# A transformer block on one core: the causal convolution by 128-column blocks, 11 of its taps on TensorE, and its layer norm in halves

## The chip, the cores and the metric

The kernel runs on one core of a Trainium2 chip. The metric is the device time of one execution in microseconds (us). The core has five engines that run side by side and meet at semaphores: TensorE (PE), VectorE (DVE), ScalarE (ACT), GpSimd (POOL) and SyncE (SP, which here only issues DMAs).

## The reference

One layer on 512 tokens of width 1024: a convolution branch and an attention branch from one projection, an output projection, and a mixture of 32 experts (each token uses 4).

```
u = rms_norm(x, norm_mix_g)
a, g, q, k, v = split(u @ w_in)                  # a and g: 512 columns each
y = causal_depthwise_conv(a * sigmoid(g), conv_w)    # 31 taps, per channel
conv_out = silu(layer_norm(y + conv_b))          # norm over the 512 channels
attn_out = diff_attention(q, k, v)               # 4 heads, 4 query blocks, 2 maps per head
h = x + concat(conv_out, attn_out) @ w_out
h = h + moe(rms_norm(h, norm_ffn_g))             # router, top 4, two matmuls per expert
```

## The kernel before

**Stages.** The program is written out by hand, engine by engine: each engine has one list of instructions in a fixed order, and semaphores hold it where it needs another's result. There are five stages.

1. *Entry.* x is loaded, normed and turned; `uT_hi` and `uT_lo` are its two parts. Every large product of the kernel is made of three matmuls, high by high, high by low and low by high (`split_mm`, L1374 to L1376), so each weight chunk of 1 MB goes through ACT (`hi_front`, L606, makes `whi`) and DVE (`lo_front`, L920, makes `wlo`) before PE can use it.
2. *Projections.* The chunks c = 0 to 9 of w_in. Chunks 0 and 2 hold the columns of a, 1 and 3 those of g, with 256 columns each, that is two blocks (o = 0 and 1) of 128 channels. The convolution has its channels on the partitions, in four such blocks; a block's gated input is `gated(c)` (L944), which needs the sigmoid on ACT (L632, L637). The four rows of the attention bias are made of the one-hot matrix on PE (`bias_row`, L1387), copied out by ACT (L618, L619), stored and loaded again by SP. Then come v (chunks 4, 5), q (6, 7) and k (8, 9).
3. *Units.* The attention has 16 units, one for each query block qb and head h, with keys of width 128 (units 0 to 3), 256 (4 to 7), 384 (8 to 11) and 512 (12 to 15). In its round i each engine does a fixed list. PE: the scores of unit i + 2 (L1473), then what stands beside unit i, then the transposes of unit i (L1550), then the values of unit i - 1 (L1532). DVE: the row maximum of unit i + 1 (L1037), the sum of one tile if there is one (L1084), the difference of the two maps of unit i (L1047 to L1055), then what stands beside it. ACT: the exponentials of unit i + 1 (L699), the copy of the turned map of unit i (L742), the output of unit i - 1 (L709, L710), then what stands beside it.
4. *Output projection.* The half that multiplies the convolution's output is eight tiles (`tile_of_conv(j)`: chunk 10 for j = 0 to 3, chunk 11 for j = 4 to 7) of 12 matmuls each, every one summed into `h1` by DVE (`add_tile(j)`). The attention's half is `out_rows(t)`, from chunks 12 and 13. Between the last values and `out_rows(0)` stand the deviation of the attention output (L752), its scaling (L1127) and its turning (L1563), split by ACT (L758) and DVE (L1132).
5. *Experts.* Routing, then a loop over expert items, each with 12 chunks of 1 MB.

**The convolution's taps.** A tap of one block on DVE is one instruction over 128 x 512 (L962, the first one of a block L958). `dve_taps` is the order of the taps, and `conv(count)` issues the next `count` of them. On PE a tap is a matmul with a diagonal matrix that ACT makes from the identity (`diagonals`, L626), and it is summed in one bank of PSUM (`conv_taps`, L1459). Before, block 3 has all its 31 taps on PE and blocks 0 to 2 theirs on DVE (93). Both run on into the units: 5 DVE taps beside each of units 0 to 3 and 1 beside unit 4, and `PE_TAPS_BESIDE` = 6, 7, 7, 7, 4 PE taps beside units 0 to 4.

**The layer norm.** Its steps stand beside units, by the constants MEAN to SPLIT: the means on PE (L1485, unit 5), the centring on DVE (L1065, 5), the squares on ACT (L716, 5), the variance on PE (L1492, 6), the deviation on ACT (L720, 6), the reciprocal and the norm on DVE (L1070, L1071, 7), SiLU and the high part on ACT (L725, L728, 7), the low part on DVE (L1075, 8). From unit 9 (`FIRST_TILE`) on one tile stands beside each unit; all but the last use one bank (`SPARE_BANK`), so a tile waits for the sum of the one before. The tile j = 7 stands behind the turning of the attention output. The bias of the experts' first product is prepared beside units 10 (DVE, L1100), 11 (ACT, L692), 12 and 13 (DVE, L1104).

```
        MEAN, CENTRE, SQUARE, VARIANCE, DEVIATION, NORM, SILU, SPLIT, FIRST_TILE = 5, 5, 5, 6, 6, 7, 7, 8, 9
        TAPS_BESIDE = 5
        CONV_BANK = [SPARE_BANK] * (2 * T - 1) + [7]
        PE_TAPS_BESIDE = (6, 7, 7, 7, 4)
```

SP starts to load the experts' weights when the values of the last unit are done.

## Time and profile before

| | us |
|---|---|
| median of 3 runs (lowest, highest) | 1468.08 (1465.13, 1468.4) |
| the profiled execution's own time | 1468.58 |
| its span, first to last instruction | 1467.0 |
| PE, DVE, ACT busy in the span | 1402.7, 1233.8, 1005.5 |
| first matmul of the projections | 19.1 |
| first tap on PE (start of unit 0) | 146.6 |
| first tile | 210.1 |
| end of the last unit's values | 248.2 |
| first transpose of `h1` | 269.6 |

A timeline row gives start, duration, engine, line, operation, what it writes and reads, shape, count, and in brackets how long the engine stood idle before it and who ended that. A row of the chain of waits gives start, duration and what was on the chain. A row of a table by stage gives the stage, then the busy time of PE, PE's weight loads, DVE, ACT and POOL (with the number of instructions), the clock that TensorE was granted as a share of 2.4 GHz, the share of DMA time and GB/s. A grouped row gives the count, the busy time in us, the mean ns of one, and the idle time before.

### The profile page before, as it was taken

To read this page: it belongs to the slowest core of one execution; us is meant where nothing else is said; L and a number is where in the kernel's file an instruction comes from. 1 tells how busy PE (TensorE), PEld (TensorE's weight loads), DVE (VectorE), ACT (ScalarE), POOL (GpSimd) and SP (SyncE) were. 2 spreads that over 40 slices of the span, in tenths; PEclk is the share of its full clock that TensorE was granted. 3 is DMA by queue.
4 is the path that set the end of the run, shared out by engine and by line. 5 is a ranking of instruction groups with operands and counts; after the bars stand their busy time and mean duration, and the time that the engine had idled before them with its cause. 6 is when DMAs were issued, how large, how long until landed. Compare 5 with 4: busy or idle time off the path is not lost.

```text
span 1467.0 us, 20156 instructions
## 1 busy us (share of the span) xinstructions
PE 1402.7 (96%) x6532; PEld 1133.0 (77%) x6532; DVE 1233.8 (84%) x1059; ACT 1005.5 (69%) x1016; POOL 265.4 (18%) x285
## 2 busy tenths in 40 slices
PE   6999968988999999999999999999999999999995
PEld 4887446876788888888888888888888888888884
DVE  4688666488899989999999999998989899899984
ACT  5248365256677777777777777777777777777773
POOL 3000000026221121111211112111121222221111
PEclk9999979999999999999999999999999999999998
DMA  8412002689999999999999999999999999999971
GB/s 245 153 56 86 15 15 74 256 287 203 411 402 391 383 378 370 368 373 371 362 379 370 366 383 361 388 357 366 379 363 372 370 365 376 375 368 370 370 284 21
DMA packets 96969, 446.78 MB, mean 305 GB/s; under 512 B 14896, under 2 KB 19008, under 8 KB 63920
## 3 DMA queue, kind: packets, MB, share of 16 engines
q1 hardware_dynamic: 82944, 422.86, 76.3%
q0 software_dynamic: 12000, 20.49, 5.4%
q10 hardware_dynamic: 2000, 3.10, 0.7%
q8 instruction: 14, 0.23, 0.1%
q14 instruction: 11, 0.09, 0.0%
HBM read 439.70 MB, written 22.43 MB: 315 GB/s over the span
## 4 chain that ended last, share of the span: by engine, by line
PE 91%; DVE 2%; DMA 2%; issue 2%; POOL 1%; ACT 1%; SPq 0%; ACTq 0%; POOLq 0%; DVEq 0%
PE psum L1374 27%; PE psum L1376 27%; PE psum L1375 26%; PE psum L1698 2%; PE psum L1459 2%; PE psum L1707 2%; POOL slot_table L512 1%; PE psum L1724 1%; DMA xg<-hn_rows,slot_i 1%; DMA ring<-in_w_in 1%; PE psum L1594 1%; PE psum L1532 0%; PE psum L1632 0%; PE psum L1473 0%; PE psum L1492 0%
## 5 line engine op out<-in xcount | busy, mean ns | idle before, releaser
L1224 DVE TENSOR_TENSOR wlo<-ring,whi 128x2048 fp32r<-128x2048 f32 x384 | 871.5, 2290 | 101.8 <-ACT whi L792 97.8
L792 ACT ACTIVATE whi<-ring 128x2048 fp32r<-128x2048 f32 x384 | 737.6, 1921 | 197.0 <-PE psum L1376 196.9
L1374 PE MATMUL psum<-whi,xT_hi 128*128 128x512 f32 x1024 | 402.2, 393 | 7.3 <-DVE xT_lo L1230 3.7
L1376 PE MATMUL psum<-wlo,xT_hi 128*128 128x512 f32 x1024 | 398.7, 389 | 0.0
L1375 PE MATMUL psum<-whi,xT_lo 128*128 128x512 f32 x1024 | 398.7, 389 | 0.0
L1374 PEld LDWEIGHTS psum<-whi,xT_hi 128*128 128x128 f32 x1024 | 192.3, 188 | 47.8 <-DVE wlo L1224 5.0
L1376 PEld LDWEIGHTS psum<-wlo,xT_hi 128*128 128x128 f32 x1024 | 192.2, 188 | 40.2
L1375 PEld LDWEIGHTS psum<-whi,xT_lo 128*128 128x128 f32 x1024 | 192.4, 188 | 38.6
L1374 PE MATMUL psum<-whi,aT_hi 128*128 128x512 f32 x512 | 202.6, 396 | 1.9 <-ACT y_sb L845 1.9
L1376 PE MATMUL psum<-wlo,aT_hi 128*128 128x512 f32 x512 | 200.0, 391 | 0.0
L1375 PE MATMUL psum<-whi,aT_lo 128*128 128x512 f32 x512 | 200.0, 391 | 0.0
L533 POOL DMA_INDIRECT out<-y_sb,slots x32 | 81.1, 2533 | 398.5 <-ACT y_sb L845 385.1
L1374 PEld LDWEIGHTS psum<-whi,aT_hi 128*128 128x128 f32 x512 | 96.6, 189 | 21.3 <-issue 2.2
L1376 PEld LDWEIGHTS psum<-wlo,aT_hi 128*128 128x128 f32 x512 | 96.4, 188 | 20.2
L1375 PEld LDWEIGHTS psum<-whi,aT_lo 128*128 128x128 f32 x512 | 96.5, 189 | 19.2
L545 POOL COPY slots_moved<-slots 128x4 int32<-128x4 int32 x30 | 30.0, 1002 | 265.9 <-DMA out<-y_sb,slots 265.9
L1374 PE MATMUL psum<-whi,uT_hi 128*128 128x512 f32 x160 | 65.2, 407 | 4.4 <-DVE uT_lo L1075 2.2
L832 ACT ACTIVATE sig<-psum 128x512 f32<-128x512 f32 x64 | 34.7, 594 | 48.4 <-PE psum L1724 48.4
L504 POOL DMA_INDIRECT xg<-hn_rows,slots x30 | 34.0, 1133 | 177.6 <-PE psum L1698 142.4
L1376 PE MATMUL psum<-wlo,uT_hi 128*128 128x512 f32 x160 | 63.7, 398 | 0.0
L1375 PE MATMUL psum<-whi,uT_lo 128*128 128x512 f32 x160 | 63.5, 397 | 0.0
L838 ACT ACTIVATE aT_hi<-psum 128x512 fp32r<-128x512 f32 x64 | 34.8, 596 | 41.2 <-PE psum L1707 41.2
(256 smaller groups left out, 1342.2 us busy)
## 6 DMA issues: line engine op xcount, KB each, us to landing
ring<-in_w_gate_up SPq DMA_DIRECT2D x256, 1024.0 KB, 7.9
ring<-in_w_down SPq DMA_DIRECT2D x128, 1024.0 KB, 7.2
ring<-in_w_in SPq DMA_DIRECT2D x10, 1024.0 KB, 12.0
ring<-in_w_out SPq DMA_DIRECT2D x4, 1024.0 KB, 5.0
h<-in_x SPq DMA_DIRECT2D x4, 512.0 KB, 5.5
hn_rows<-hn ACTq DMA_DIRECT2D x4, 512.0 KB, 2.6
out<-h POOLq DMA_DIRECT2D x4, 512.0 KB, 11.1
bias_rows<-rows_st SPq DMA_DIRECT2D x1, 1280.0 KB, 4.8
```

The costliest lines, as they stand in the source:

```text
L504: pool.indirect_dma_start(out=xg[:, :], out_offset=None, in_=hn_rows, in_offset=bass.IndirectOffsetOnAxis(ap=index, axis=0), bounds_check= ...
L533: pool.indirect_dma_start(out=out, out_offset=bass.IndirectOffsetOnAxis(ap=slots[:, place, 0:1], axis=0), in_=y_sb[:, :], in_offset=None, ...
L545: COPY(slots_moved[:, :, token], slots[:, 1:5, token]).then_inc(move_step, 1)
L792: nc.scalar.activation(whi[:, hi_of(number), :], ring[:, slot(number), :], ACT.Copy).then_inc(hi_ready, 1)
L832: nc.scalar.activation(sig[:, cols], bank(2 * half, 2).rearrange("p (f two) -> p two f", two=2)[:, 0, :], ACT.Silu, scale=ALPHA).then_inc( ...
L838: nc.scalar.activation(aT_hi[:, half * 4:half * 4 + 4, :], bank(6 + half), ACT.Copy, scale=1.0 / ALPHA).then_inc(aT_hi_done, 1)
L1224: TT(wlo[:, slot(number), :], ring[:, slot(number), :], whi[:, hi_of(number), :].bitcast(F32), ALU.subtract).then_inc(lo_ready, 1)
L1374: MM(o, s_hi, m_hi, start=first, stop=False)
L1375: MM(o, s_lo, m_hi, start=False, stop=False)
L1376: return MM(o, s_hi, m_lo, start=False, stop=last)
L1459: ins = MM(bank(SPARE_BANK), diag[:, n, :], u_pad[:, 3, n:n + S], start=(n == 0), stop=(n == PE_TAPS - 1))
L1698: ins = nc.tensor.transpose(bank(6 + half)[:, k * P:(k + 1) * P], xg[:, (half * 4 + k) * P:(half * 4 + k + 1) * P], ident[:, :])
```

## The change

**a and g by blocks.** PE no longer takes chunk by chunk but block by block: a's block 0, g's block 0, a's block 1, g's block 1, then the bias rows, then the same for blocks 2 and 3. ACT's sigmoids and DVE's `gated` follow one by one, and DVE's taps start right behind the first. `dve_taps` gets a new order (block 0 alone for 13 taps, then pairs of neighbouring blocks). SP's load of chunk 6 stands behind the bias rows as before.

**11 taps of block 3 on PE, 20 on DVE.** `PE_TAPS` goes from 31 to 11 (the last 11 taps), 3, 3, 3 and 2 beside units 0 to 3. DVE has 113 taps; 4 beside each of units 0 to 2, the other 9 beside unit 3, where the bank of PE's taps is added too.

**The layer norm** stands beside later units, and centring, squares, norm, SiLU, high and low parts are done for tokens 0 to 255 and 256 to 511 one after the other: means at unit 5, centring 6, squares 7, variance and deviation 9, norm 10 and 11, SiLU 12, low part 13. **The tiles** start at unit 14: tiles 0 and 1 stand beside units 14 and 15, the other six between the last values and the turning of the attention output, over three banks. Chunk 12's low part is made among their sums, chunk 13's high part behind the deviation of the attention output. **The up bias's steps** stand beside units 11, 13, 14 and 15.

```diff
-PE_TAPS = TAPS
+PE_TAPS = 11
...
-        MEAN, CENTRE, SQUARE, VARIANCE, DEVIATION, NORM, SILU, SPLIT, FIRST_TILE = 5, 5, 5, 6, 6, 7, 7, 8, 9
-        TAPS_BESIDE = 5
-        CONV_BANK = [SPARE_BANK] * (2 * T - 1) + [7]
-        PE_TAPS_BESIDE = (6, 7, 7, 7, 4)
+        CONV_END, MEAN, CENTRE, SQUARE, VARIANCE, DEVIATION, NORM, SILU, SPLIT, FIRST_TILE = 3, 5, 6, 7, 9, 9, 10, 12, 13, 14
+        TAPS_BESIDE = 4
+        HALVES = (slice(0, S // 2), slice(S // 2, S))
+        BESIDE_TILES = H * T - FIRST_TILE
+        CONV_BANK = [SPARE_BANK] * BESIDE_TILES + [(SPARE_BANK, 6, 7)[j % 3] for j in range(2 * T - BESIDE_TILES)]
+        PE_TAPS_BESIDE = (3, 3, 3, 2)
...
+                for half, cols in enumerate(HALVES):
+                    act.wait_ge(normed, half + 1)
+                    for c in range(4):
+                        nc.scalar.activation(ln_tmp[:, c, cols], acc[:, c, cols], ACT.Silu, bias=ln_b[:, c:c + 1],
+                                             scale=ln_g[:, c:c + 1]).then_inc(silu_done, 1)
+                    act.wait_ge(silu_done, 4 * (half + 1))
+                    nc.scalar.activation(uT_hi[:, 0:4, cols], ln_tmp[:, :, cols], ACT.Copy).then_inc(conv_hi, 1)
...
+            block_of(0, 0)
...
+            block_of(1, 0)
+            block_of(0, 1)
+            block_of(1, 1)
+            pe.wait_ge(tab_ready, H)
+            pe.wait_ge(cw_ready, 1)
+            pe.wait_ge(conv_in, 1)
+            for h in range(H):
+                bias_row(h)
+            pe.wait_ge(brow_evac, 1)
+            block_of(2, 0)
+            pe.wait_ge(brow_evac, 3)
+            block_of(3, 0)
+            pe.wait_ge(brow_evac, 4)
+            block_of(2, 1)
+            block_of(3, 1)
...
-            for j in range(len(units) - FIRST_TILE, 2 * T - 1):
+            for j in range(BESIDE_TILES, 2 * T):
                 tile_of_conv(j)
```

What stands in a row on the engines. First DVE in the projections (`u_pad` is `gated`, `acc` a tap, `wlo` a chunk's low part). Before:

```order
L937 COPY cw_sb<-psum 128x124
L938 TENSOR_SCALAR vecs<-vecs 128x1
L939 TENSOR_TENSOR rw<-rw,vecs 128x256
L920 TENSOR_TENSOR wlo<-ring,whi 128x2048
L944 TENSOR_TENSOR u_pad<-psum,sig_g 128x512 x2
L958 TENSOR_SCALAR acc<-u_pad,cw_sb,vecs 128x512 x2
L962 SCALAR_TENSOR_TENSOR acc<-u_pad,cw_sb,acc 128x512 x2
L920 TENSOR_TENSOR wlo<-ring,whi 128x2048
L962 SCALAR_TENSOR_TENSOR acc<-u_pad,cw_sb,acc 128x512 x6
L920 TENSOR_TENSOR wlo<-ring,whi 128x2048
L962 SCALAR_TENSOR_TENSOR acc<-u_pad,cw_sb,acc 128x512 x11
```

After:

```order
L950 COPY cw_sb<-psum 128x124
L951 TENSOR_SCALAR vecs<-vecs 128x1
L952 TENSOR_TENSOR rw<-rw,vecs 128x256
L956 TENSOR_TENSOR u_pad<-psum,sig_g 128x512
L970 TENSOR_SCALAR acc<-u_pad,cw_sb,vecs 128x512
L974 SCALAR_TENSOR_TENSOR acc<-u_pad,cw_sb,acc 128x512 x3
L933 TENSOR_TENSOR wlo<-ring,whi 128x2048
L974 SCALAR_TENSOR_TENSOR acc<-u_pad,cw_sb,acc 128x512 x9
L956 TENSOR_TENSOR u_pad<-psum,sig_g 128x512
L974 SCALAR_TENSOR_TENSOR acc<-u_pad,cw_sb,acc 128x512
L970 TENSOR_SCALAR acc<-u_pad,cw_sb,vecs 128x512
L974 SCALAR_TENSOR_TENSOR acc<-u_pad,cw_sb,acc 128x512 x3
```

The first gated block stands alone now, with four of its taps ahead of chunk 3's low part and nine behind it; the second gated block follows these.

Then PE in the units, from the end of the taps to the tile or the mean (`psum<-ident,pd` are the transposes, `psum<-v_tok,pdT` the values, `psum<-kT_hi,qT_hi` scores, `psum<-acc,inv_dc` the means). Before, rounds 4 to 6:

```order
L1459 MATMUL psum<-u_pad,diag 128x512 x4
L1550 MATMUL psum<-ident,pd 128x128 x2
L1532 MATMUL psum<-v_tok,pdT 128x128
L1473 MATMUL psum<-kT_hi,qT_hi 128x256 x2
L1473 MATMUL psum<-kT_hi,qT_lo 128x256 x2
L1473 MATMUL psum<-kT_lo,qT_hi 128x256 x2
L1485 MATMUL psum<-acc,inv_dc 128x512 x4
L1550 MATMUL psum<-ident,pd 128x128 x2
L1532 MATMUL psum<-v_tok,pdT 128x128 x2
L1473 MATMUL psum<-kT_hi,qT_hi 128x384 x2
L1473 MATMUL psum<-kT_hi,qT_lo 128x384 x2
L1473 MATMUL psum<-kT_lo,qT_hi 128x384 x2
```

After, rounds 3 to 5:

```order
L1496 MATMUL psum<-u_pad,diag 128x512 x2
L1581 MATMUL psum<-ident,pd 128x128
L1563 MATMUL psum<-v_tok,pdT 128x128
L1510 MATMUL psum<-kT_hi,qT_hi 128x256 x2
L1510 MATMUL psum<-kT_hi,qT_lo 128x256 x2
L1510 MATMUL psum<-kT_lo,qT_hi 128x256 x2
L1581 MATMUL psum<-ident,pd 128x128 x2
L1563 MATMUL psum<-v_tok,pdT 128x128
L1510 MATMUL psum<-kT_hi,qT_hi 128x256 x2
L1510 MATMUL psum<-kT_hi,qT_lo 128x256 x2
L1510 MATMUL psum<-kT_lo,qT_hi 128x256 x2
L1520 MATMUL psum<-acc,inv_dc 128x512 x4
```

The means stand behind the scores of unit 7 as before, but no taps stand in round 4 any more, and the variance, which stood in round 6, stands in round 9.

Last DVE behind the last unit (`stat<-stat` and `o_tok` scale the attention output, `h_87<-psum,h_87` is `add_tile`, `uT_lo<-psum,vecs,uT_hi` the low part of the turned output, `wlo` chunk 12 or 13). Before:

```order
L1055 RECIPROCAL inv_sum<-att 128x1
L1123 RECIPROCAL stat<-stat 128x16
L1124 TENSOR_SCALAR stat<-stat 128x16
L1127 TENSOR_TENSOR o_tok<-o_tok,stat 128x512 x4
L1084 TENSOR_TENSOR h_87<-psum,h_87 128x512
L1132 SCALAR_TENSOR_TENSOR uT_lo<-psum,vecs,uT_hi 128x4x128 x4
L920 TENSOR_TENSOR wlo<-ring,whi 128x2048
L1084 TENSOR_TENSOR h_87<-psum,h_87 128x512
```

After:

```order
L1126 TENSOR_TENSOR b_split<-b_raw,b_split 32x2048
L1106 TENSOR_TENSOR h_87<-psum,h_87 128x512
L1146 RECIPROCAL stat<-stat 128x16
L1147 TENSOR_SCALAR stat<-stat 128x16
L1150 TENSOR_TENSOR o_tok<-o_tok,stat 128x512 x4
L1106 TENSOR_TENSOR h_87<-psum,h_87 128x512 x4
L933 TENSOR_TENSOR wlo<-ring,whi 128x2048
L1106 TENSOR_TENSOR h_87<-psum,h_87 128x512 x2
L1159 SCALAR_TENSOR_TENSOR uT_lo<-psum,vecs,uT_hi 128x4x128 x4
L933 TENSOR_TENSOR wlo<-ring,whi 128x2048
```

One sum behind the scaling has become six, with a chunk's low part among them, and none stands behind the turned output.

## Rows read from the trace of the kernel before

**Rows 1.** The page's part 4: the chain that ended last, by engine.
```profile
PE 91%; DVE 2%; DMA 2%; issue 2%; POOL 1%; ACT 1%; SPq 0%; ACTq 0%; POOLq 0%; DVEq 0%
```
**Rows 2.** Table by stage: projections, units 0 to 4, norm, tiles, behind the units.
```profile
19.10:146.60 127.50, 124.03 (x550) 100.28 (x550) 93.27 (x131) 63.70 (x210) 0.00 (x0) 0.96 0.34 115
146.60:180.50 33.90, 33.83 (x107) 16.25 (x107) 21.75 (x63) 9.96 (x37) 0.00 (x0) 0.94 0.00 1
180.50:215.60 35.10, 21.69 (x81) 13.62 (x80) 22.40 (x49) 22.77 (x49) 0.00 (x0) 0.71 0.13 31
215.60:248.20 32.60, 30.34 (x178) 24.44 (x176) 21.02 (x49) 19.44 (x51) 0.15 (x1) 1.00 0.00 1
248.20:269.60 21.40, 17.61 (x78) 14.28 (x79) 12.00 (x18) 6.38 (x12) 0.00 (x0) 0.92 0.95 382
```
**Rows 3.** Timeline of DVE in the projections, rows with idle time before them.
```profile
40.43 2.29 DVE L920 TENSOR_TENSOR wlo<-ring,whi 128x2048 fp32r<-128x2048 f32 x1 [6.64 <-ACT whi L606]
...
50.86 1.29 DVE L944 TENSOR_TENSOR u_pad<-psum,sig_g 128x512 f32<-128x512 f32 x2 [8.14 <-ACT sig_g L632]
...
97.65 2.29 DVE L920 TENSOR_TENSOR wlo<-ring,whi 128x2048 fp32r<-128x2048 f32 x1 [3.05 <-ACT whi L606]
```
**Rows 4.** Timeline of DVE and PE in units 0 to 4.
```profile
151.05 0.28 DVE L1037 CUSTOM_DVE_ANT_0 prob<-psum,bias_raw 128x128 f32<-128x128 f32 x1
...
152.31 3.39 DVE L962 SCALAR_TENSOR_TENSOR acc<-u_pad,cw_sb,acc 128x512 f32<-128x512 f32 x5
...
168.73 6.28 PE L1459 MATMUL psum<-u_pad,diag 128*128 128x512 f32 x14
...
179.57 0.75 DVE L1061 TENSOR_SCALAR acc<-psum,vecs 128x512 f32<-128x512 f32 x1 [7.83 <-PE psum L1459]
```
**Rows 5.** The chain of waits, from the centring to the tiles (210.13: first tile).
```profile
184.19 2.30 DVE acc L1065
...
188.47 5.25 PE psum L1492 x8
...
195.16 1.28 ACT L720
...
197.17 3.36 DVE std L1070
...
202.88 2.94 ACT ln_tmp L725 x4
205.84 1.92 ACT uT_hi L728
...
210.13 0.79 PE psum L1374
...
211.35 0.43 PE psum L1376
...
222.82 0.23 PE psum L1375
```
**Rows 6.** Groups of instructions by line and shape, 144 to 249 us.
```profile
L1037 DVE CUSTOM_DVE_ANT_0 prob<-psum,bias_raw 128x512 f32<-128x512 f32 x8 | 5.2, 688 | 0.2
...
L1485 PE MATMUL psum<-acc,inv_dc 128*128 128x512 f32 x8 | 3.7, 605 | 0.0
```
**Rows 7.** Table by stretch, columns as in rows 2: TensorE's clock around pauses.
```profile
184.90:188.30 3.40, 0.65 (x6) 0.32 (x6) 3.26 (x10) 2.46 (x4) 0.00 (x0) 0.99 0.24 48
188.30:191.70 3.40, 3.23 (x4) 1.51 (x5) 1.95 (x8) 1.11 (x5) 0.00 (x0) 0.51 0.00 0
...
246.50:249.90 3.40, 1.62 (x14) 1.43 (x13) 0.00 (x0) 2.85 (x8) 0.00 (x0) 1.00 0.17 36
```
**Rows 8.** The chain of waits, last values and first transpose of h1.
```profile
246.28 1.86 PE psum L1532 x16
...
269.57 0.87 PE psum L1586 x8
```
**Rows 9.** Timeline of DVE behind the units.
```profile
256.78 2.28 DVE L920 TENSOR_TENSOR wlo<-ring,whi 128x2048 fp32r<-128x2048 f32 x1
```

More of the change, by code:

```diff
@@ L1458, in conv_taps @@
                     pe.wait_ge(diag_ready, n + 1)
[L1459 removed]
+                    ins = MM(bank(SPARE_BANK), diag[:, n, :], u_pad[:, 3, n + TAPS - PE_TAPS:n + TAPS - PE_TAPS + S], start=(n == 0), stop=(n == PE_TAPS - 1))
                 tap += count
@@ L1514, in tile_of_conv @@
                 half_rows(bank(CONV_BANK[j]), c, j % T, tile_done if j % T < T - 1 else chunk_used)
-            def means():
-                for c in (3, 2, 0, 1):
-                    mean_part(c)
-            beside = {MEAN: means, VARIANCE: variance}
+            beside = {MEAN: mean, VARIANCE: variance}
             scores(0)
```

201 lines of the change are left out of this document (104 added, 97 removed).

## The prediction

> **What bounds the kernel now.** I read the page's chain first: PE is on it for 91% of the span [rows 1]. The expert loop, from 368.6 us on, is not touched by the change, so I cut the part ahead of it into stages [rows 2] and asked in each what PE does. In the projections PE is busy 124.0 of 127.5 us: PE is the bound and DVE has room, 93.3 of 127.5. In units 0 to 4 PE is busy 33.83 of 33.90, nearly all of it with taps. In the layer norm (180.5 to 215.6) PE is busy 21.7 of 35.1 at a mean clock of 0.71: there a single chain over three engines is the bound. In the tile stage PE is at 30.3 of 32.6 with the full clock. Behind the units PE is busy 17.6 of 21.4. So a gain can come from taps taken off PE in units 0 to 4, from the norm's chain laid beside attention work, and in the tail, which must take the tiles that the units no longer hold.
>
> All my times below count from the profiled execution (1468.58 us, span 1467.0). Its own time is 0.5 us above the median of the runs, 1468.08, so I subtract 0.5 at the end.
>
> **Part 1, projections: nothing on the path.** DVE gets 20 more taps there and in the units: 113 in place of 93. By the new counts 92 stand ahead of the units, before it was 72, so all 20 land in the projections. One costs 0.66 to 0.68 us in a run of taps of different blocks (five take 3.39) [rows 4], so 20 x 0.66 = 13.2 us. The first 13 taps of block 0 each follow the one they depend on, so the overlap of about 0.1 us is lost: 1.4 more, 14.6 in all. Against this stand DVE's idle times of 6.64, 8.14 and 3.05 us, the last up to 97.65 [rows 3], 17.8 together, and some smaller ones. Walking the new order: a's and g's block 0 are done on PE near 32.8, the first taps run from 34.2, chunk 3's low part is ready at 42.5 and wanted at 53.7 (behind the bias rows), chunk 5's at 70.6 and wanted at 82.7; chunk 8's low part is still set by ACT at 97.65, and DVE's last tap ahead of it ends at 96.6. PE waits for none of them. The bias rows move from 32.9 to 43.8 with SP's store, its reload and chunk 6's load behind them, 11 us later; chunk 6 (12 us to land) is then there near 67 and ACT takes it at 72.6. Value: 0, range -1 to +3 (the slack at 96.6 is only 1 us).
>
> **Part 2, units up to the first tile.** Before: 146.6 to 210.1, 63.5 us. After, piece by piece:
> - Units 0 to 3 become DVE's. A unit's attention work on DVE is 1.26 us at width 128 (151.05 to 152.31) [rows 4], about 1.7 at 256. Behind unit 0's difference (147.75) stand 4 + 4 + 4 + 9 = 21 taps, 21 x 0.66 = 13.9, two units of 1.26, one of 1.7 and the sum of PE's bank, 0.75 as L1061 [rows 4]: 166.6 us. Before, that point was 180.2 (L1061 starts at 179.57 behind 7.83 idle). PE's 11 taps take 11 x 0.89 = 9.8 (7 take 6.28) [rows 4] and hide. Gain so far 13.6.
> - Units 4 and 5 bring scores for the means at 169.9. The means took 3.7 us (eight passes) [rows 6] with PE warm and the variance's eight 5.25 behind a pause [rows 5]. PE has now been idle some 5 us in unit 3, so I take 5.25: 175.2. Centring is 2.3 as before [rows 5], in two halves 2.4: 177.7.
> - Units 7 to 9 run under it. ACT's squares (two halves of 1.0) hold the exponentials of unit 9 to 184.2; the variance runs 183.4 to 187.1; then ACT's copy and output, a table load 1.28 and the root 0.69 [rows 5]: 190.7.
> - The norm's first half is 1.7 (half of 3.36) [rows 5] and 1.2, to 193.6; unit 12's row maximum and unit 11's difference 2.4 (a row maximum is 0.69 for each of two maps at width 512) [rows 6], to 196.0; the second half 2.9; the bias's step 0.6; then one more row maximum, its exponentials on ACT, which take about as long, copy and output: 203.7.
> - SiLU is a lump on ACT. Before 2.94 + 1.92 and a table load [rows 5]; now 1.28 + 2 x (2.07 + 1.06) = 7.5, since eight instructions of half the width and two copies carry their fixed parts twice. 211.3, and the low part's second half 1.25: the first tile at 212.6.
>
> So 66.0 us where there were 63.5, but with unit 13's work done and not unit 8's.
>
> **Part 3, first tile to the last values.** Before 210.1 to 248.2 = 38.0 us [rows 5, 8], seven tiles. Now two tiles and units 14 and 15. The first tile runs at 0.43 us a pass (211.35) [rows 5], 12 passes, 5.3 us with its start, since PE has waited through SiLU as it did before; beside it ACT does the bias's high part (1.9) ahead of unit 15's exponentials, DVE two low parts (2.3 each). Tile 1 waits for tile 0's sum at 220.1, ends at 222.9; transposes, copy and values: 225.2. That is 12.6 us.
>
> **Part 4, behind the values.** Before 248.2 to 269.6 = 21.4 us [rows 8]. Now six tiles stand first on PE, 72 passes of 0.23 (222.82) [rows 5], 16.4; they hide the root and the scaling of the attention output, for which PE waited before (part of its 3.8 idle) [rows 2]. Then the turning, about 1.1, with ACT's split and DVE's low part of the first (1.7 from the end of the tiles). `out_rows(0)`'s first half would run from +18.1 to +20.8, but chunk 13's low part comes behind four turned parts as before (256.78 to 259.06) [rows 9], now at +20.1 to +22.4, and no tile stands between: PE waits 1.6. Three more halves: +30.6. This costs 9.2 us.
>
> **Sum.** 146.6 + 66.0 + 12.6 + 30.6 = 255.8 for the point that was 269.6: -13.8. To this I add 1.8 for what the walk leaves out: hops between engines and passes at half clock in units 6 to 13. -12.0. What follows (routing, gather, loop) hangs on `h1` and on the chunk counts, all of which shift along. 1468.6 - 12.0 - 0.5 = 1456.1 us.
>
> **The clock.** The rows show what I fear most. From 184.9 to 188.3 PE worked 0.65 us, and the next stretch was granted 0.51, that is 1.2 GHz; yet from 246.5 to 249.9, with 1.62 us of work, the clock stayed at 1.00 [rows 7]. In units 6 to 13 PE will work 1.3 to 2.2 us of each unit's 2.5 to 3.3, close between these. The Trainium skill, in "TensorE: Matmul & The Clock Gate", section "A second HAM failure mode: psum-queue depth-cycling", says that a matmul stream with frequent small gaps makes the clock swing between its two levels. It speaks for the first rival below. By it the sum would be 1464 and not 1456; by the row at 246.5 there would be no swing. The rows above bear both.
>
> **Rivals.**
> - *Half clock through the sparse units.* For: the row at 188.3, and the norm stage's mean of 0.71 [rows 2]. Against: the row at 246.5. Price: means and variance at 6.8 us each (eight passes; the 0.43 pass of rows 5 is of rounded inputs, a full one takes two of them) in place of 5.25 and 3.7, 4.7 us; units 8 to 13 with a round of 3.1 to 4.4 us on PE in place of ACT's 2.4 to 3.2, about 1 us each, 5. Less the 1.8 that I have: +8, 1464.
> - *The same clock also in the tail: slower than before.* If the six tiles and the four half rows did not get the full clock either, 120 passes would cost 0.43 for 0.23 us [rows 5], 24 us, and with the first rival's 8 the time is 1488; the kernel is slower by 0.3% as soon as 43 of these passes stay slow (1464 + 43 x 0.2 = 1472.6). Against: every run of dense tiles before got back to 1.00 within some 5 us in the tile stage [rows 2].
> - *The gain is not passed on.* SP's weight loads start when the values end, 23 us earlier, so they lie elsewhere against the small transfers of routing. If a gather lands as late as before, up to all of it goes: 1461 to 1468. Against: the loads behind the sixth are held by chunks that PE frees in the same place.
> - *The lumps overlap better.* Warm means (-1.6), no cost of hops (-1.8), and unit 12's difference and the first half's low part under SiLU (-2): 1450.
>
> **Chances.** The forecast (1452 to 1461) 0.62; overlap better 0.12; half clock in the units 0.14; not passed on 0.06; the tail's clock or a late chunk in the projections, slower 0.06. A measurement can tell about 0.3% (4.4 us) from no change, so the bound is 1463.7. Faster: 0.62 + 0.12 + half of 0.14 and of 0.06 = 0.84; within 0.3% the other halves, 0.10; slower 0.06. Range 1449 to 1465: it reaches down past the fourth rival and up past the first, and leaves out the slower case and what little lies beyond on either side, some 0.12.
>
> **What would show it.** In the changed profile: PE's first tap still near 146.6 (part 1); L1078 on DVE near 166 (part 2); the last of the norm's chain, L1097, ending near 212.6, with a PE clock above 0.8 between 175 and 203; SP's first expert load at 225 to 227 (part 3); the first transpose of `h1` 30.6 us later, near 257 (part 4), and a wait of PE for L933 inside `out_rows(0)`; everything after it at the old distance. The prediction fails if the first tap comes later than 149, if the norm's chain ends past 220, or if the transposes of `h1` start less than 8 us earlier but the end doesn't follow.

## The result, and the profile after

The changed kernel takes 1456.38 us (median of 4 runs, 1456.13 to 1458.91) against 1467.78 of the kernel before on the same chip: a ratio of 0.9935, with a 95% interval from 0.9923 to 0.9948. By the ratio that is 9.5 us less, by the two medians 11.4. The forecast was 1456.1, range 1449 to 1465, faster. The profiled execution has a span of 1454.8 us against 1467.0, 12.2 less; the kernel before was profiled in an execution slower than each of its four timed ones (1468.58 us), so this difference is somewhat large. In the rest of the text every number is of one profiled execution, unless it is called a median or a ratio.

The table by stage, cut where the prediction's parts end (its columns are those of [rows 2]; the stages are the projections, units 0 to 3, the units up to the first tile, the first tile to the last values, and what lies behind the values up to the first transpose of `h1`):

```profile
19.10:147.80 128.70, 124.82 (x550) 100.12 (x550) 107.26 (x151) 58.16 (x190) 0.00 (x0) 0.95 0.33 113
147.80:167.90 20.10, 15.91 (x56) 7.83 (x56) 19.64 (x54) 8.28 (x30) 0.00 (x0) 0.84 0.01 1
167.90:214.40 46.50, 29.04 (x148) 19.50 (x148) 31.69 (x91) 34.71 (x89) 0.00 (x0) 0.79 0.10 23
214.40:227.40 13.00, 11.13 (x58) 9.46 (x59) 9.64 (x17) 8.34 (x23) 0.15 (x1) 0.88 0.00 1
227.40:258.30 30.90, 29.48 (x138) 24.07 (x137) 16.87 (x23) 8.05 (x13) 0.00 (x0) 1.00 0.72 289
```

Against [rows 2]: DVE has 107.26 us of work in the projections instead of 93.27, and PE's stage is hardly longer (128.7 against 127.5). Units 0 to 3, with DVE busy 19.64 of 20.10, take 20 us where PE's taps held units 0 to 4 for 34. Then follow 46.5 us in which no engine is full: PE 29.0, DVE 31.7, ACT 34.7. Last comes a dense tail, PE 29.5 of 30.9 at the full clock.

DVE in the projections, timeline rows with the idle time ahead of them (these answer [rows 3]):

```profile
33.22 0.69 DVE L956 TENSOR_TENSOR u_pad<-psum,sig_g 128x512 f32<-128x512 f32 x1 [4.50 <-ACT sig_g L630]
39.98 2.29 DVE L933 TENSOR_TENSOR wlo<-ring,whi 128x2048 fp32r<-128x2048 f32 x1 [3.01 <-ACT whi L611]
...
98.79 2.29 DVE L933 TENSOR_TENSOR wlo<-ring,whi 128x2048 fp32r<-128x2048 f32 x1 [1.14 <-ACT whi L611]
```

The first gated block now comes at 33.2 and not at 50.9, and the three gaps of 6.64, 8.14 and 3.05 us have shrunk to 4.50, 3.01 and 1.14. The taps went into them.

The end of unit 3 on DVE, and PE's next instruction (timeline):

```profile
160.92 6.28 DVE L974 SCALAR_TENSOR_TENSOR acc<-u_pad,cw_sb,acc 128x512 f32<-128x512 f32 x9
167.30 0.69 DVE L1078 TENSOR_TENSOR acc<-acc,psum 128x512 f32<-128x512 f32 x1
```

```profile
169.64 0.69 PE L1581 MATMUL psum<-ident,pd 128*128 128x128 f32 x2 [5.92 <-DVE pd L1069]
```

The sum with PE's bank (L1078) starts at 167.30; its counterpart stood at 179.57 [rows 4]. PE has been done with its 11 taps for 5.9 us.

The chain of waits from there to the second tile (start, duration, what was on the chain); it answers [rows 5]:

```profile
171.69 4.38 PE psum L1520 x8
...
184.29 3.63 PE psum L1526 x8
...
206.97 2.08 ACT ln_tmp L739 x4
209.07 1.06 ACT uT_hi L742
...
217.10 1.81 ACT b_split L704
...
218.94 2.28 DVE b_split L1126
...
222.00 0.50 PE psum L1400
```

The means (L1520) and the variance (L1526) are there, then SiLU and its high part (L739, L742). Behind the first tile, which starts at 214.5, the chain doesn't run over PE but over the bias's high part on ACT (L704) and a low part on DVE (L1126): `add_tile(0)` stands in DVE's list behind it, and PE, done with the tile, its transposes and values, is idle for 1.8 us ahead of tile 1 (L1400, 222.00).

The tail, one row of DVE's and one of PE's timeline:

```profile
247.51 2.28 DVE L933 TENSOR_TENSOR wlo<-ring,whi 128x2048 fp32r<-128x2048 f32 x1
```

```profile
249.85 0.50 PE L1400 MATMUL psum<-whi,uT_hi 128*128 128x512 f32 x1 [1.16 <-DVE wlo L933]
```

This is chunk 13's low part, and PE waiting for it inside `out_rows(0)`.

### The profile page after: what moved, and what is told of

The parts are those of the page before. It is cut to its first block, busy times and chain, and to the rows that moved or that the text cites. A ratio compares the mean times of both kernels' runs of the same rounds, so it can differ in the third digit from the quotient of the medians.

```text
span 1454.8 us, 20088 instructions
## 1 busy us (share of the span) xinstructions
PE 1386.8 (95%) x6492; PEld 1126.4 (77%) x6492; DVE 1248.9 (86%) x1083; ACT 1000.9 (69%) x1003; POOL 269.9 (19%) x285
## 4 chain that ended last, share of the span: by engine, by line
PE 89%; DVE 4%; ACT 2%; DMA 2%; issue 2%; POOL 2%; SPq 0%; POOLq 0%; ACTq 0%; DVEq 0%
PE psum L1400 27%; PE psum L1401 27%; PE psum L1402 27%; PE psum L1730 2%; PE psum L1739 2%; POOL slot_table L517 1%; PE psum L1756 1%; DMA xg<-hn_rows,slot_i 1%; DVE acc L974 1%; DMA ring<-in_w_in 1%; PE psum L1626 1%; DVE prob L1053 0%; PE psum L1664 0%; PE psum L1563 0%; DVE wlo L933 0%
## 5 line engine op out<-in xcount | busy, mean ns | idle before, releaser
L1400 PE MATMUL psum<-whi,xT_hi 128*128 128x512 f32 x1024 | 402.2, 393 | 7.2 <-DVE xT_lo L1256 3.7
L1400 PEld LDWEIGHTS psum<-whi,xT_hi 128*128 128x128 f32 x1024 | 192.3, 188 | 47.7 <-DVE wlo L1250 4.9
L1400 PE MATMUL psum<-whi,aT_hi 128*128 128x512 f32 x512 | 202.7, 396 | 1.9 <-ACT y_sb L858 1.9
L1400 PEld LDWEIGHTS psum<-whi,aT_hi 128*128 128x128 f32 x512 | 96.5, 188 | 21.4 <-issue 2.2
L1401 PEld LDWEIGHTS psum<-whi,aT_lo 128*128 128x128 f32 x512 | 96.6, 189 | 19.3
L974 DVE SCALAR_TENSOR_TENSOR acc<-u_pad,cw_sb,acc 128x512 f32<-128x512 f32 x109 | 75.3, 743 | 0.5
L550 POOL COPY slots_moved<-slots 128x4 int32<-128x4 int32 x30 | 26.8, 895 | 262.1 <-DMA out<-y_sb,slots 262.1
L1400 PE MATMUL psum<-whi,uT_hi 128*128 128x512 f32 x160 | 64.2, 401 | 9.3 <-DVE uT_lo L1097 6.1
L509 POOL DMA_INDIRECT xg<-hn_rows,slots x30 | 33.2, 1107 | 177.3 <-PE psum L1730 141.2
```

Of the source, the lines that this page charges most:

```text
L509: pool.indirect_dma_start(out=xg[:, :], out_offset=None, in_=hn_rows, in_offset=bass.IndirectOffsetOnAxis(ap=index, axis=0), bounds_check= ...
L974: STT(out=acc[:, c, :], in0=u_pad[:, c, w:w + S], scalar=cw_sb[:, c, w:w + 1], in1=acc[:, c, :], op0=ALU.mult, op1=ALU.add).then_inc(conv_ ...
L1400: MM(o, s_hi, m_hi, start=first, stop=False)
L1401: MM(o, s_lo, m_hi, start=False, stop=False)
```

## The experiments

Twelve runs were made, in three groups of four, each group on one chip beside runs of the kernel before. To compare executions I use four marks: PE's first tap, the first tile, the end of the last values, and the first transpose of `h1`; all in us, read off the timeline of each. The last column is the span behind the transpose. The marks are of one execution each, and it need not be a typical one: in e_warm and e_best13 it was the fastest of the four.

| kernel | ratio to before, 95% interval | first tap | tap to first tile | tile to last values | values to `h1` | sum from the tap | behind `h1` |
|---|---|---|---|---|---|---|---|
| before | 1 | 146.7 | 63.4 | 38.1 | 21.2 | 122.7 | 1197.6 |
| changed | 0.9935 (0.9923, 0.9948) | 147.8 | 66.7 | 12.8 | 30.9 | 110.4 | 1196.6 |
| after_again | 0.9942 (0.9929, 0.9954) | 147.3 | 68.7 | 12.9 | 30.8 | 112.4 | 1196.8 |
| u_norm | 0.9940 (0.9927, 0.9954) | 147.0 | 55.5 | 36.9 | 20.7 | 113.1 | 1195.8 |
| u_taps | 0.9999 (0.9990, 1.0009) | 147.3 | 75.6 | 12.8 | 30.8 | 119.2 | 1197.2 |
| u_blocks | 0.9952 (0.9937, 0.9967) | 152.9 | 67.3 | 12.8 | 30.8 | 110.9 | 1194.3 |
| e_bias | 0.9916 (0.9901, 0.9931) | 146.6 | 67.8 | 11.4 | 30.9 | 110.1 | 1195.5 |
| e_all | 0.9896 (0.9881, 0.9912) | 147.4 | 65.0 | 12.5 | 29.4 | 106.9 | 1196.7 |
| e_warm | 0.9933 (0.9913, 0.9953) | 146.8 | 64.7 | 12.9 | 30.8 | 108.4 | 1197.1 |
| n_halves | 0.9929 (0.9913, 0.9945) | 148.2 | 51.0 | 38.4 | 20.4 | 109.8 | 1198.6 |
| n_best | 0.9934 (0.9921, 0.9948) | 148.2 | 54.1 | 35.9 | 20.6 | 110.6 | 1196.8 |
| t_13 | 0.9923 (0.9910, 0.9935) | 148.0 | 65.7 | 12.8 | 30.9 | 109.4 | 1196.8 |
| e_best | 0.9891 (0.9876, 0.9905) | 148.0 | 65.5 | 9.7 | 29.3 | 104.5 | 1195.8 |
| e_best13 | 0.9885 (0.9871, 0.9899) | 148.2 | 62.6 | 9.7 | 29.4 | 101.7 | 1195.6 |

**Theory and rival.** The marks of before and after already suggested where the gain is. From the end of the taps' sum to the transposes of `h1` it is 89.3 us before (180.2 to 269.6) and 90.4 after (167.9 to 258.3). So my theory was: all of the gain is taps that PE no longer does in units 0 to 4, and the norm spread over the units gives nothing by itself. The rival: the spread norm carries a good part of it. Two kernels, each with one of the two alone (the blocks in the projections are in both), tell them apart.

### u_norm: the taps without the spread norm

```
-        CONV_END, MEAN, CENTRE, SQUARE, VARIANCE, DEVIATION, NORM, SILU, SPLIT, FIRST_TILE = 3, 5, 6, 7, 9, 9, 10, 12, 13, 14
+        CONV_END, MEAN, CENTRE, SQUARE, VARIANCE, DEVIATION, NORM, SILU, SPLIT, FIRST_TILE = 3, 5, 5, 5, 6, 6, 7, 7, 8, 9
```

The steps at full width, the tiles, chunks 12 and 13 and the bias are as before as well.

> The changed kernel with the layer norm, the tiles, chunks 12 and 13 and the bias's steps put back as they stood in the kernel before (whole width, units 5 to 8, tiles from unit 9 on); kept are the blocks in the projections and the 11 taps on TensorE. Theory (the whole gain is taps taken off TensorE in units 0 to 3, the spread norm gives nothing): the sum of the taps' bank ends at 168 as in the changed kernel; unit 4 now stands alone behind it (3 us), then the 89.3 us of the kernel before, so the first transpose of h1 comes at 260.2 against 258.3, and the time is 1456 to 1459 us. Rival (a good part of the gain comes from the norm laid beside the units): 1462 us or more, and the transposes of h1 behind 264.

Measured: the transposes start at 260.1, median 1457.44, ratio 0.9940. The theory said 260.2. That it is met to 0.1 us is partly luck: the taps' sum ended at 167.1 and not at 168, and from there to the transposes it was 93.0 us and not 92.3, with means of 5.59 us where the kernel before had 3.7 [rows 6]. The chain of waits shows the old norm at its new place:

```profile
170.77 5.59 PE psum L1507 x8
...
180.67 5.40 PE psum L1513 x8
...
202.49 0.79 PE psum L1387
```

Its first tile (L1387) starts at 202.5, twelve us ahead of the changed kernel's, but eight tiles still come, and units 9 to 13 are yet to be done, which the changed kernel has behind it by its first tile.

### u_taps: the spread norm without the taps

```
-PE_TAPS = 11
+PE_TAPS = TAPS
-        CONV_END, MEAN, CENTRE, SQUARE, VARIANCE, DEVIATION, NORM, SILU, SPLIT, FIRST_TILE = 3, 5, 6, 7, 9, 9, 10, 12, 13, 14
+        CONV_END, MEAN, CENTRE, SQUARE, VARIANCE, DEVIATION, NORM, SILU, SPLIT, FIRST_TILE = 4, 5, 6, 7, 9, 9, 10, 12, 13, 14
-        PE_TAPS_BESIDE = (3, 3, 3, 2)
+        PE_TAPS_BESIDE = (6, 7, 7, 7, 4)
```

> The changed kernel with all 31 taps of block 3 back on TensorE in units 0 to 4 (6, 7, 7, 7, 4 as before); kept are the blocks in the projections, the norm in halves over the units and the tail. Theory (the taps carry the gain): TensorE's taps run to 181, L1078's counterpart ends there, and the first transpose of h1 comes 268 to 270; 1466 to 1469 us. Rival (the spread norm carries a good part of it): 1462 us or less.

Measured: the taps' sum at 180.3, the transposes at 266.5, median 1466.0 over ten runs, ratio 0.9999. As a whole, the theory's number. From the first tap to `h1` the profile shows 3.5 us less than in the kernel before. One reason stands in its chain of waits:

```profile
181.30 3.64 PE psum L1520 x8
...
193.17 3.63 PE psum L1526 x8
```

With PE busy up to 181, means and variance both run at the full clock, 3.6 us each, where the kernel before had 3.7 and 5.25 [rows 5, 6]. Of these 3.5 us the ten runs show nothing in the time. So the blocks and the spread norm together are worth 0 within the 1.4 us of that interval. u_norm says the same of the spread norm from the other side, within some 2 us: 0.9940 without it, 0.9935 and 0.9942 with it. The marks lean a little towards the spread norm there too (113.1 us from the tap to `h1` without it, 110.4 and 112.4 with it); the times don't show it.

### u_blocks: are the blocks needed?

a and g whole chunk by whole chunk again, with the taps still on DVE:

```
-            block_of(0, 0)
...
-            block_of(1, 0)
-            block_of(0, 1)
-            block_of(1, 1)
...
+            for c in range(4):
+                pe.wait_ge(lo_ready, c + 1)
...
+                for o in range(2):
...
             gated(0)
+            gated(1)
             conv(4)
```

> The changed kernel with the projections of a and g whole chunk by whole chunk as before (bias rows behind chunk 0, gates of blocks 0 and 1 together near 54 us), with the 20 more taps kept on VectorE. Theory (the blocks make the room: VectorE's first tap comes 15 to 20 us later, so its work no longer ends in time for the low parts of chunks 6 to 9): TensorE waits for them, the first TensorE tap comes at 150 to 156 instead of 147.8, 1458 to 1464 us. Rival (VectorE had room enough anyway, and the blocks only cost the 12 half-clock passes behind the bias rows): first tap at 146 to 147, 1455 us.

Measured: first tap at 152.9, median 1459.24, ratio 0.9952. The forecast of the time and of the tap holds, but not the place. PE's waits in the projections:

```profile
PE psum L1411 <- DVE qk_tok L977: 5.9, 2, 4.9
```

PE waits 5.9 us for q and k scaled by DVE (L977, in the changed kernel L984), which stand in DVE's list behind the taps; the changed kernel has 1.1 us of this wait. It does not wait for any chunk's low part. So the blocks make the room for 20 more taps, worth 5 us at the first tap. In the ratio (0.9952 against 0.9935 and 0.9942) only some 2 us are seen, and the intervals overlap: behind `h1` this execution is 2.3 us shorter (1194.3 against 1196.6), for a reason that stays open. So the 5 us at the tap are shown, a gain of the blocks in the time is not.

### e_bias: the bias's steps where their engines wait

```
-                      SQUARE: square_centred, DEVIATION: deviation, SILU: silu, BIAS + 2: bias_high}
+                      SQUARE: square_centred, DEVIATION: deviation, SILU: silu, BIAS: bias_high}
...
-            beside = {BIAS: one_more, BIAS + 3: lambda: bias_low(slice(E, 2 * E)), BIAS + 4: lambda: bias_low(slice(3 * E, P)),
-                      CONV_END: conv_end, CENTRE: centre, NORM: lambda: norm(0), SPLIT: conv_lo}
+            beside = {BIAS - 2: one_more, BIAS + 1: lambda: bias_low(slice(E, 2 * E)),
+                      CONV_END: conv_end, CENTRE: centre, NORM: lambda: norm(0), SPLIT: lambda: (bias_low(slice(3 * E, P)), conv_lo())}
```

> The changed kernel with the up bias's steps put where their engines wait for the norm: the one added at unit 9 on VectorE, the high part at unit 11 on ScalarE, the two low parts at units 12 and 13 (ahead of the norm's own low part). Theory (the bias's steps at units 14 and 15 lie on the chain between the first tile and the last values, 1.9 us on ScalarE and 2 x 2.3 on VectorE): the stretch from the first tile to the last values goes from 13.0 to 9 to 11 us, 1452 to 1454.5 us. Rival (TensorE's tiles and clock set that stretch, the bias lies beside them): 1456 us as before the edit. A second rival: the high part delays SiLU, the first tile moves later by 2, and nothing is gained.

Measured: median 1453.62, ratio 0.9916; the first tile to the last values takes 11.4 us instead of 12.8. The chain of waits behind the first tile now runs over PE:

```profile
213.12 1.24 DVE uT_lo L1097
214.40 0.79 PE psum L1400
...
217.32 0.43 PE psum L1400
218.60 0.35 PE psum L1400
```

The bias is off the chain, but most passes of the first tile run at 0.43 us (5.0 us for the twelve), so the gain stops at 1.4 us: what is late next is PE with its own clock. The sum from the tap (110.1 against 110.4) shows hardly any of it, since in this execution the means took 5.59 us and not 4.38. The step in the ratio, 0.0019 to 0.0026 or 2.8 to 3.8 us, is larger than what the profile accounts for; the intervals overlap, so I take the 1.4 as shown and no more.

### e_warm: useless matmuls against the half clock

```
+                if i == FIRST_TILE:
+                    for n in range(4):
+                        MM(bank(SPARE_BANK), ident[:, :], acc[:, 0, :], start=True, stop=True)
...
+                if i == CONV_END + 1:
+                    pe.wait_ge(pdT_evac, i)
+                    for n in range(4):
+                        MM(bank(TURN_BANK), ident[:, :], u_pad[:, 3, 0:S], start=True, stop=True)
```

> The changed kernel with eight useless matmuls more: four of 1.2 us in TensorE's idle 5.9 us ahead of the means, four in its idle 6.1 us ahead of the first tile; nothing else is changed. Theory (half clock behind a pause costs real time there): the means take 3.7 instead of 4.4 us, the first tile of 12 passes 2.8 instead of 4.2; the span shrinks by 1.5 to 2.5 us, 1454 us. Rival (the clock isn't bought back by work that waits in between, or the useless work ends late and delays): no gain, or slower by 1 to 2 us.

Measured: the means take 3.65 us, and the sum from the tap is 108.4, 2.0 less than in the changed kernel's first execution. The profiled execution is the fastest of four; the median is 1456.68 with runs from 1453.96 to 1459.75, so the time itself doesn't decide it. Nor do the warm means repeat: e_best, below, has the same useless matmuls ahead of them. Ahead of the first tile the useless work failed, which the table by stretch shows (the first tile starts at 211.5):

```profile
206.00:209.00 3.00, 3.00 (x8) 1.14 (x6) 1.23 (x1) 2.97 (x6) 0.00 (x0) 1.00 0.00 0
209.00:211.50 2.50, 0.20 (x1) 0.00 (x0) 1.26 (x2) 2.45 (x3) 0.00 (x0) 1.00 0.00 0
211.50:214.50 3.00, 2.98 (x8) 2.35 (x9) 2.45 (x8) 2.99 (x10) 0.00 (x0) 0.57 0.00 0
```

PE was full at 1.00 until 209, then idle for 2.3 us, and the tile began at 0.57 on average. From the first tile to the last values it is 12.9 us as without the useless work. I expect that a warm tile would have given nothing here either, since the bias's steps set that stretch (the chain of waits has them behind the tile as above, and PE idle for 1.6 us ahead of tile 1); no run has a warm tile with the bias at its old place.

### e_all: three moves

The bias as in e_bias; chunk 12's low part at unit 8 on DVE, chunk 13's in the tail at chunk 12's place; tiles 0 and 1 wait for the norm's first half alone:

```
-                      CONV_END: conv_end, CENTRE: centre,
+                      CONV_END: conv_end, 8: lambda: lo_front(12), CENTRE: centre,
...
                 add_tile(j)
-            lo_front(12)
+            lo_front(13)
...
-                if j == 0:
-                    pe.wait_ge(mix_conv, 2)
+                if j in (0, T // 2):
+                    pe.wait_ge(mix_conv, 2 * j // T + 1)
```

> The changed kernel with three small moves at once: the bias's steps as in e_bias; chunk 12's low part at unit 8 on VectorE and chunk 13's in the tail where chunk 12's stood (so it is ready before the turned parts); tiles 0 and 1 wait only for the norm's first half. Theory: 1.6 us between first tile and last values (as e_bias showed), 1.3 us of TensorE's wait for chunk 13's low part in the tail, 0 to 1 from the first tile; the tail behind the last values goes from 31.0 to 29.6 us; 1451 to 1453 us. Rival (chunk 12's low part at unit 8, 2.3 us of VectorE, lands on the norm's chain, and the first tile comes later by as much): 1453.5 to 1455 us.

Measured: median 1452.35, ratio 0.9896; values to `h1` 29.4 us as expected, and PE's wait for a low part in the tail is gone. All that is left of waits there is:

```profile
PE psum L1399 <- DVE uT_lo L1159: 0.3, 1, 0.3
```

Tap to first tile is 65.0 although its means ran wholly at half clock (5.86 us), for the tile now waits for the first half alone. That moves the mark: the stretch from the first tile to the last values (12.5 us) begins earlier and can't be compared with that of e_bias (11.4). A mark that stands still is the end of the norm's last high part on ACT (L742 in the changed kernel). From there to the last values:

| kernel | last high part ends | to last values |
|---|---|---|
| changed, after_again, e_warm, t_13 | 213.2, 214.7, 210.2, 212.4 | 14.1 in each |
| e_bias | 213.1 | 12.7 |
| e_all | 214.1 | 10.8 |
| e_best | 212.2 | 11.0 |
| e_best13 | 209.6 | 10.9 |

So the three moves take 3.3 us out of this stretch, 1.4 of them the bias's and 1.9 more the tile's early start. In e_all the first tile's passes run at half clock as in e_bias, and now it costs nothing, since the chain runs beside them, over ACT and DVE to the transposes of unit 14:

```profile
213.04 1.06 ACT uT_hi L742
214.11 1.28 ACT L711
...
217.47 0.76 DVE pd L1069
218.28 0.66 PE psum L1580 x4
```

### n_halves and n_best: a compact norm in halves

If the spread gives nothing, a compact norm whose halves overlap should beat both. n_halves is u_norm with the steps in halves:

```
-                      CONV_END: conv_end, CENTRE: centre, NORM: norm, SPLIT: conv_lo, SPLIT + 1: lambda: lo_front(12)}
+                      CONV_END: conv_end, CENTRE: centre, NORM: lambda: (norm(0), norm(1)), SPLIT: conv_lo, SPLIT + 1: lambda: lo_front(12)}
```

> u_norm (norm compact over units 5 to 8, tiles from unit 9) with the norm's steps in halves one right behind the other, and tiles 0 and 1 waiting for the first half only. Theory (halves shorten the chain only when they overlap on two engines: squares under centring, SiLU under the norm's second half, the first tile under the low part's second half): from the end of the means to the first tile 26.1 us in u_norm become 20 to 21; the tiles stage keeps its length, so the transposes of h1 move from 260.1 to 255, 1452 us. Rival (tiles 0 and 1 start earlier but the two bias steps and the units set the end of the stage): 1455 to 1457 us.

n_best also moves the bias into the norm:

```
-                      SQUARE: square_centred, DEVIATION: deviation,
+                      SQUARE: lambda: (bias_high(), square_centred()), DEVIATION: deviation,
...
-                      CONV_END: conv_end, CENTRE: centre,
+                      CONV_END: conv_end, CENTRE: lambda: (one_more(), centre(), bias_low(slice(E, 2 * E))),
```

> n_halves with the up bias's steps moved into the norm's waits: the one added ahead of the centring, the high part ahead of the squares (ScalarE waits there for the centring), the low parts behind the centring and at unit 6. Theory: 4 to 5 us less in the tile stage than n_halves (1.8 us on ScalarE and 2 x 2.3 on VectorE lie on the chain there in u_norm), at 0 to 1 us more in the norm: 1447 to 1449 us, faster than the kernel before and the changed one. Rival (the bias steps in the norm delay it by what they save behind it): 1452 us as n_halves.

Both forecasts failed: medians 1457.95 and 1457.25, ratios 0.9929 and 0.9934. In n_halves the norm's chain did shrink, from 26.1 to 21.6 us between the means and the first tile. But the stage behind it grew from 36.9 to 38.4; why is not resolved. From n_halves to n_best the norm lost 3.1 us and the tile stage won 2.5, as the rival had it. The loss is in the timeline of PE, the variance of n_halves (here its first two passes) and of n_best:

```profile
181.09 1.12 PE L1521 MATMUL psum<-ln_tmp,inv_dc 128*128 128x512 f32 x2 [2.15 <-ACT ln_tmp L729]
```

```profile
181.51 6.44 PE L1521 MATMUL psum<-ln_tmp,inv_dc 128*128 128x512 f32 x8 [3.76 <-ACT ln_tmp L729]
```

With the high part ahead of the squares PE rests for 3.76 us and not 2.15, and the eight passes that follow take 6.4 us and not 3.7: 4.3 us more, of which shorter means (4.4 against 5.6 us) gave 1.2 back. Why the tile stage won 2.5 (1.0 against u_norm) and not 4 to 5, the table by stage of n_best says:

```profile
167.60:202.30 34.70, 20.07 (x75) 11.78 (x75) 24.26 (x51) 22.91 (x49) 0.00 (x0) 0.70 0.14 31
202.30:238.20 35.90, 34.14 (x191) 27.37 (x189) 22.59 (x60) 22.04 (x63) 0.15 (x1) 0.97 0.00 1
```

Between first tile and last values PE is busy 34.1 of 35.9 us. With a unit and a tile in each round PE is the bound, and much of the bias's 6.4 us on ACT and DVE had lain beside it. In the changed kernel that stage has two tiles only, and there the bias does lie on the chain. I had carried a price from the one schedule to the other.

The last column holds one more surprise: n_halves takes 2.8 us more than u_norm behind `h1`. PE's waits between 270 and 400 us show one for the gather of expert rows in that kernel, and so do those of before (3.0 us), changed (2.2), e_all and n_best (2.4 each); the other nine executions have none. It doesn't settle the column: the changed kernel has 1196.6 us with the wait and, as after_again, 1196.8 without it.

```profile
PE psum L1723 <- DMA xg<-hn_rows,slot_i: 2.8, 1, 2.8
```

### t_13, e_best, e_best13 and the changed kernel again

t_13 gives two taps back to PE, which has 5.9 us of rest in unit 3:

```
-PE_TAPS = 11
+PE_TAPS = 13
-        PE_TAPS_BESIDE = (3, 3, 3, 2)
+        PE_TAPS_BESIDE = (3, 3, 3, 4)
```

> The changed kernel with 13 taps on TensorE instead of 11 (the last four in unit 3), 111 instead of 113 on VectorE. Theory (VectorE sets the end of units 0 to 3, TensorE has 5.9 us of rest behind its taps): VectorE ends 1.3 us earlier, TensorE's rest shrinks to some 2 us, so the means run at the full clock, 3.7 instead of 4.4 to 5.9: from the first tap to the transposes of h1 110.4 us become 107 to 109; 1453.5 to 1455 us. Rival (TensorE was full until 163.7, and its two more taps hold unit 3's transposes and the sum): 110 to 112, 1456 to 1458 us.

Measured: the taps' sum starts 17.9 us behind the first tap instead of 19.5, so DVE did set the end of these units. The sum from the tap is 109.4; PE's rest shrank to 2.6 us, and the means still took 5.34 us, so the clock fell all the same. Median 1455.72, ratio 0.9923: the sign is as expected, its size not above the scatter.

e_best is e_all with the useless matmuls:

> e_all and the eight useless matmuls of e_warm together. Theory (the two are independent: one takes steps off the chain, the other keeps the full clock behind two pauses): from the first TensorE tap to the transposes of h1 106.9 us in e_all become 103.5 to 105.5 (means 3.7 for 5.9, two scores and transposes 0.8 less, the first tile about 1 less); 1449.5 to 1451.5 us. Rival (in e_all the pause ahead of the first tile is shorter, and the useless matmuls end after the first half is ready): 106 to 107, 1452 us.

Measured: 104.5 us from the tap, median 1449.86, ratio 0.9891. The expectation has the time right and the pieces wrong. The means took 4.41 us and not 3.7, with the same useless matmuls ahead of them that had gone with 3.65 in e_warm; that is 1.5 less than e_all's, another 1.1 lies between the means and the last high part, and the first tile gave nothing (11.0 us behind the last high part against 10.8 in e_all). e_best13 is e_all with 13 taps and only the useless matmuls ahead of the first tile:

> e_all with 13 taps on TensorE, and of the useless matmuls only the four ahead of the first tile. Theory (real taps serve as well as useless matmuls to hold the clock, and relieve VectorE by 1.3 us): first tap to transposes of h1 102.5 to 104.5 us; 1448.5 to 1450.5 us. Rival (as for t_13): 105 to 107, 1451.5 to 1453 us.

Measured: 101.7 us, median 1448.80, ratio 0.9885. It is the fastest of all, 16.9 us below the kernel before and 9.5 below the changed one in the same group (1458.25). The intervals of e_all, e_best and e_best13 overlap (0.9896, 0.9891, 0.9885), so what the last two add to e_all is not shown in the time. In the marks it lies ahead of the first tile: the taps' sum comes 1.3 us sooner behind the tap than in e_all, and the means end 3.0 us sooner behind that sum. But t_13 has the same edit up to there, and both rest for 2.6 us ahead of the transposes that lead to the means; here e_best13, then t_13:

```profile
168.62 0.44 PE psum L1583 x2
...
169.84 3.65 PE psum L1519 x8
```

```profile
168.19 0.44 PE psum L1581 x2
...
169.41 5.34 PE psum L1520 x8
```

So 1.7 of these 3.0 us are the clock's scatter and not the edit's, and taps don't hold the clock as surely as the expectation had it. Around e_best13's first tile, by stretch:

```profile
204.00:207.70 3.70, 2.85 (x13) 2.85 (x14) 3.60 (x5) 3.67 (x7) 0.00 (x0) 0.58 0.00 0
207.70:211.30 3.60, 3.60 (x9) 1.55 (x9) 2.44 (x3) 3.54 (x5) 0.00 (x0) 0.95 0.00 0
211.30:214.10 2.80, 2.80 (x15) 2.25 (x14) 2.01 (x8) 2.80 (x11) 0.00 (x0) 1.00 0.00 0
```

and in DVE's timeline (the low part that the tile waits for) and the chain of waits:

```profile
207.22 1.23 DVE L1097 TENSOR_TENSOR uT_lo<-ln_tmp,uT_hi 128x1024 fp32r<-128x1024 f32 x1
```

```profile
207.68 3.67 PE psum L1576 x8
211.35 0.23 PE psum L1399
```

Here the useless work (L1576) runs right up to the tile, and the 12 passes take 2.8 us instead of 5.0. But the tile's low part was there at 208.45: the useless work is now on the chain itself and holds the tile back by more than 2 us. What the warm passes win, it costs. The first tile to the last values is 9.7 us in both kernels against 12.5 in e_all, and that number misleads: it is the tile that starts later, for from the last high part it is 10.9 and 11.0 against 10.8.

The changed kernel once more, unaltered:

> The changed kernel itself, unaltered, on the same chip as the three above, to see what of the stages repeats from one execution to another. Theory: its time and its norm's chain repeat within 0.3%, but the passes at half clock do not fall on the same places (means 4.4 to 5.9 us, first tap 146.6 to 148.2); 1456 us. Rival: the clock's pattern is fixed by the program, and means 4.4 and first tap 147.8 come again.

Measured: median 1458.25, ratio 0.9942. Its chain of waits:

```profile
171.11 5.87 PE psum L1520 x8
...
185.21 3.63 PE psum L1526 x8
```

The means took 5.87 us and not 4.38, the first tap came at 147.3 and not 147.8: the same program, with its half-clock passes at other places. The clock's pattern is not fixed by the program.

## Why the prediction was right, point by point

- **Part 1, projections, 0 (range -1 to +3).** The first tap came at 147.8 and 147.3, 0.6 to 1.1 us later than 146.7. No wait for a low part appeared. Over the twelve executions with this order in the projections the tap lies between 146.6 and 148.2. The clock behind the bias rows, which the term did not have, may be part of that: from 44 to 54 us it is 0.66 here and 0.83 in e_bias, e_warm and u_norm, whose taps come at 146.6, 146.8 and 147.0. But n_halves has 0.83 too, and 148.2; the cause stays open. The margin of 1 us that I saw at 96.6 held: DVE still waits 1.14 us for ACT at 98.79.
- **Part 2, units 0 to 3: 20.0 us from the first tap to the end of the sum.** Measured 20.1, against 33.6 before. This is the term that makes the gain, 13.6 forecast and 13.5 measured from the tap, and u_norm and u_taps confirm that it stands alone: with the taps and the old norm 0.9940, with the new norm and the old taps 0.9999.
- **Part 2, norm.** Means 5.25 forecast, 4.38 and 5.87 in two executions; variance 3.7, measured 3.63 both times; SiLU's lump 7.5, measured 7.5 (205.67 to 213.2). Tap to first tile 66.0, measured 66.7 and 68.7, with the 1.8 allowance not counted in. With it the forecast would be 67.8, between the two. The variance's 3.63 us also speak against the first rival, which had priced it at 6.8.
- **Part 3: 12.6.** Measured 12.8 to the last values' end. The walk let tile 1 wait for tile 0's sum until 7.5 us behind the tile's start, and 7.5 was measured (214.49 to 222.00), so the wait was priced. But it named the high part and the two low parts as lying "beside" the first tile; in fact the high part and the first low part were the chain, and PE was idle for 1.8 us ahead of tile 1. Right number, wrong owner; the chain of waits and e_bias showed it.
- **Part 4: 30.6, with 1.6 of PE waiting for chunk 13's low part.** Measured 30.9 with 1.2 of waiting. e_all took the wait out and got 29.4.
- **Sum: -12.0 for `h1`.** Measured -11.3 in the profile: the tap came 1.2 us later than forecast, the three parts took 0.7, 0.2 and 0.3 longer, and the allowance of 1.8 covers most of these 2.4. The span went down by 12.2; behind `h1` it is 1.0 us less, within what this stretch varies by among executions of kernels that don't differ there (1194.3 to 1198.6). The rival that the gain is not passed on had the opposite sign in mind.
- **The time: 1456.1.** That the median of 1456.38 is 0.3 us from it is luck. The same kernel's median was 1458.25 in the last group, and by the two ratios (0.9935 and 0.9942) the gain is 9.5 and 8.5 us, where the forecast had 12.0 and so lies just beyond both intervals, though its range holds them.
- **The clock.** The granted clock is 1.00 through the tail (227.4 to 258.3), so the slow rival fell. Between 167.9 and 214.4 the mean is 0.79, and passes at 1.2 GHz lie over the means and at the first tile; from 175 to 203, where I had asked for more than 0.8, it is 0.88. The section "A second HAM failure mode: psum-queue depth-cycling" of the Trainium skill's "TensorE: Matmul & The Clock Gate" tells of one kernel whose matmul groups stand apart by short idle stretches, and there the clock swings between the two levels; the trace agrees that it swings, between 0.50 (167.5 to 171.0) and 1.00 (227.4 to 258.3). From the tap to the first tile the forecast was met within 0.7 us in one execution and exceeded by 2.7 in the other, where the means alone took 1.5 us longer, not by the 8 of the rival. Many of the slow passes lay where ACT and DVE set the pace (PE is busy 29.0 of those 46.5 us).

The forecast's weak point is its first paragraph, which names the norm laid beside attention work as a source of gain of its own. Its sum already said otherwise: the parts give -13.8, and 13.6 of that are the taps. The spread norm earned nothing that the times show: what it saves of idle time ahead of the tiles is what the tail pays for six tiles alone.

## What to carry to other kernels

Ask of each part of a change what it gives alone; here one of two large rewrites gave everything, and two marks in the trace (the end of the taps' sum and the turn of `h1`, 89.3 us apart before and 90.4 after) said so before any experiment. A step is priced by what is late beside it in that schedule: the same bias steps cost 1.4 us where a stage held two tiles, and 2.5 of their 6.4 where PE was nearly full, which moving them into the norm then took back. The half clock has such a price too: the first tile's slow passes lay on the chain in e_bias and beside it in e_all. And measure a stretch between marks that the edit doesn't move. From the first tile to the last values useless matmuls seemed to win 2.8 us (e_all to e_best); from the end of the norm's last high part they win nothing, because they had delayed the tile.
